# Rotary halves of the sparse and the odd block: exchanged by a signed permutation on TensorE, or by DMAs between rows

## The reference

```python
def apply_rope(x, cos, sin):
    half = x.shape[-1] // 2          # 32 of a head's 64
    x1, x2 = x[..., :half], x[..., half:]
    return jnp.concatenate([x1 * cos - x2 * sin, x2 * cos + x1 * sin], axis=-1)
...
q = apply_rope(rmsnorm(q.reshape(B, S, N_HEADS, HEAD_DIM), q_g), cos, sin)      # 16 heads
k = apply_rope(rmsnorm(k, k_g)[:, :, None, :], cos, sin)[:, :, 0]
qi = apply_rope(qi.reshape(B, S, IDX_HEADS, IDX_DIM), cos_i, sin_i)             # 8 index heads
ki = apply_rope(ki[:, :, None, :], cos_i, sin_i)[:, :, 0]
```

## Time and profile before

| | |
|---|---|
| median of 3 runs | 3494.64 us |
| lowest and highest | 3492.76, 3498.55 us |
| span of the profiled execution | 3495.7 us, 1.1 us above the median and within the runs |
| TensorE busy | 3254.3 us, 93% of the span |
| VectorE, ScalarE, GpSimd busy | 1721.7, 1278.4, 1177.5 us |
| mean granted TensorE clock | 0.969 of full speed |
| stage `dsa` | about 648 to 944 us of the span |
| stage `odd` | about 2720 to 2886 us of the span |

### The profile page before, as it was taken

One profiled execution on the slowest core, in us unless ns is written; L12 is line 12 of the kernel. 1 busy time (PEld: TensorE's weight loads), 2 busy tenths in 40 slices (PEclk: granted clock), 3 DMA queues, 4 the chain that ended last, 5 costly groups with the idle time before them and its releaser, 6 DMA issues.

```text
span 3495.7 us, 44614 instructions
## 1 busy us (share of the span) xinstructions
PE 3254.3 (93%) x18228; PEld 2555.2 (73%) x18228; DVE 1721.7 (49%) x3140; ACT 1278.4 (37%) x2273; POOL 1177.5 (34%) x963
## 2 busy tenths in 40 slices
PE   7999999887899997989899988999999998999998
PEld 3346888655678886755688876888887777868886
DVE  6754446588476676624566544122223318741223
ACT  2413223347432235625523234212113436743222
POOL 0233444542144442221265323223222342044443
PEclk9999999998999998999999999999999999999999
DMA  7513555310155542100122120111111111012221
GB/s 298 196 72 149 206 207 206 129 49 1 73 197 207 206 184 104 49 26 1 42 52 52 47 85 36 61 73 49 73 54 68 55 49 67 1 66 99 98 99 73
DMA packets 82412, 337.23 MB, mean 96 GB/s; under 512 B 46432, under 2 KB 50208, under 8 KB 57376
## 3 DMA queue, kind: packets, MB, share of 16 engines
q1 hardware_dynamic: 81344, 332.14, 25.7%
q10 hardware_dynamic: 864, 2.24, 0.2%
HBM read 326.64 MB, written 7.70 MB: 96 GB/s over the span
## 4 chain that ended last, share of the span: by engine, by line
PE 72%; DVE 14%; ACT 5%; POOL 3%; DMA 2%; issue 2%; SPq 1%; POOLq 0%; DVEq 0%; ACTq 0%
PE PSB L676 17%; PE PSB L680 17%; PE PSB L677 17%; PE PSB L1272 2%; PE PSB L1294 2%; PE PSB L1281 2%; PE PSB L563 2%; DVE SB L2064 2%; DVE SB L396 1%; DMA SB<-in_ada 1%; DVE SB L1366 1%; PE PSB L1833 1%; DVE PSB L1018 1%; DVE SB L1382 1%; DVE R L1024 1%
## 5 line engine op out<-in xcount | busy, mean ns | idle before, releaser
L680 PE MATMUL PSB<-R,WSR 128*128 128x512 f32 (+1 forms) x3084 | 1014.1, 366 | 0.0
L621 POOL TENSOR_TENSOR WSR<-SB,ahead 128x1024 fp32r<-128x1024 f32 x182 | 436.1, 2397 | 708.0 <-ACT ahead L598 672.6
L676 PE MATMUL PSB<-R,ahead 128*128 128x512 f32 (+1 forms) x1664 | 612.3, 368 | 2.5 <-POOL WSR L621 2.4
L677 PE MATMUL PSB<-R,ahead 128*128 128x512 f32 (+1 forms) x1664 | 592.7, 366 | 0.0
L680 PEld LDWEIGHTS PSB<-R,WSR 128*128 128x128 f32 x3084 | 533.0, 189 | 65.4
L676 PEld LDWEIGHTS PSB<-R,ahead 128*128 128x128 f32 x1664 | 312.9, 188 | 73.9 <-issue 3.5
L621 POOL TENSOR_TENSOR WSR<-SB,ffn_weights 128x1024 fp32r<-128x1024 f32 x96 | 230.0, 2396 | 388.7 <-ACT ffn_weights L598 388.7
L677 PEld LDWEIGHTS PSB<-R,ahead 128*128 128x128 f32 x1664 | 313.1, 188 | 52.8 <-issue 0.7
L676 PE MATMUL PSB<-R,ffn_weights 128*128 128x512 f32 x868 | 324.6, 374 | 7.2 <-POOL WSR L621 7.2
L677 PE MATMUL PSB<-R,ffn_weights 128*128 128x512 f32 x868 | 317.2, 373 | 0.0
L598 ACT ACTIVATE ahead<-SB 128x1024 fp32r<-128x1024 f32 x164 | 172.8, 1055 | 347.1 <-PE PSB L680 262.9
(11 more groups left out here) (441 smaller groups left out, 5763.1 us busy)
## 6 DMA issues: line engine op xcount, KB each, us to landing
SB<-in_w SPq DMA_DIRECT2D x95, 2048.0 KB, 7.5
SB<-in_ada SPq DMA_DIRECT2D x96, 1024.0 KB, 5.0
SB<-gate_rows SPq DMA_DIRECT2D x12, 512.0 KB, 4.0
SB<-in_rpb SPq DMA_DIRECT2D x8, 448.0 KB, 3.8
spill<-SB SPq DMA_DIRECT2D x1, 3072.0 KB, 9.6
SB<-gate_rows SPq DMA_DIRECT2D x24, 128.0 KB, 3.9
SB<-spill SPq DMA_DIRECT2D x1, 3072.0 KB, 9.9
SB<-in_x SPq DMA_DIRECT2D x8, 256.0 KB, 6.6
```

The lines of the kernel that those rows point to most:

```text
L621: e.tt(lr, t, hf, ALU.subtract).then_inc(*G.up(("lo", self.e0 + j)))
L676: e.mm(b[:, 0:n], wh, xh[:, lo:lo + n], x == 0, False)
L677: e.mm(b[:, 0:n], wh, xl[:, lo:lo + n], False, False)
L680: ins = e.mm(b[:, 0:n], wl, xh[:, lo:lo + n], False, last)
```

## The change

The permutation on TensorE goes, and with it the product or copy out of the bank. In its place SP issues four DMAs for each rotation, each of which copies 32 rows of the input tile (64 KB) to the partner's rows of `T`. The sign moves into the table of sines, which the host makes. `rot.dve` now multiplies `T` in place; in `dsa` from rotation 5 on POOL does it alone. `rot.pool` and `rot.dve` wait for the four DMAs to land. SP's program has the DMAs of rotation i between the calls of `panels`, and waits there until the input of the rotation is ready and until rotation i-2 is summed.

```diff
-        ropes += [np.cos(a4), np.sin(a4)]
+        ropes += [np.cos(a4), np.where(p[:, None] % 64 < 32, -1.0, 1.0) * np.sin(a4)]
...
         class Rotation:
-            def pe(self, e, P, i):
-                st = self.st
-                if i:
-                    e.wait_ge(*st.at("turn_sin", i - 1))
-                e.wait_ge(*self.ready(i))
-                e.mm(self.b, K["rot64"], self.xs[i][:, 0:S]).then_inc(*P.up(("turn", i)))
...
-            def act(self, e, A, i):
-                st = self.st
-                e.wait_ge(*st.at("turn", i))
-                if i >= len(self.T):
-                    e.wait_ge(*st.at("turned", i - len(self.T)))
-                e.act(self.T[i % len(self.T)], self.b, ACT.Copy).then_inc(*A.up(("turn_sin", i)))
...
+            def landed(self, i):
+                return self.swapped[i % len(self.T)], 64 * (i // len(self.T) + 1)
+
+            def sp(self, e, i):
+                st = self.st
+                e.wait_ge(*self.ready(i))
+                if i >= len(self.T):
+                    e.wait_ge(*st.at("turned", i - len(self.T)))
+                for o in range(0, 128, 64):
+                    for to, of in ((o, o + 32), (o + 32, o)):
+                        e.load(self.T[i % len(self.T)][to:to + 32, :], self.xs[i][of:of + 32, 0:S]).then_inc(
+                            self.landed(i)[0], 16)
+
+            def dve(self, v, D, i):
+                t = self.T[i % len(self.T)]
+                v.wait_ge(*self.landed(i))
+                v.tt(t, t, self.sin, ALU.mult).then_inc(*D.up(("turn_sin", i)))
+
+            def pool(self, e, G, i, alone=False):
+                st, x, t = self.st, self.xs[i][:, 0:S], self.T[i % len(self.T)]
+                e.wait_ge(*self.landed(i))
+                e.tt(x, x, self.cos, ALU.mult).then_inc(*G.up())
+                if alone:
+                    e.tt(t, t, self.sin, ALU.mult).then_inc(*G.up())
+                else:
+                    e.wait_ge(*st.at("turn_sin", i))
                 e.wait_ge(*G.now())
...
+                e.tt(x, x, t, ALU.add).then_inc(*G.up(("turned", i)))
...
@@ dsa, sp @@
-                for mt in order[:5] + [14] + order[5:]:
+                for s, mt in enumerate(order[:5]):
                     panels(e, "b_in", 7, mt)
-                for mt in range(8):
+                    rot.sp(e, s)
+                panels(e, "b_in", 7, 14)
+                for s, mt in enumerate(order[5:]):
+                    panels(e, "b_in", 7, mt)
+                    if s == 3:
+                        rot.sp(e, 5)
+                    if s >= 5:
+                        rot.sp(e, s + 1)
+                panels(e, "b_out", 7, 0)
+                for i in range(10, 14):
+                    rot.sp(e, i)
+                for mt in range(1, 8):
                     panels(e, "b_out", 7, mt)
...
@@ dsa, pe, att @@
-                    if i < 4:
-                        rot.pe(e, P, 10 + i)
                     if i == 3:
                         e.wait_ge(*st.at("head_ln", 8, 0))
-                    elif i == 4:
-                        e.wait_ge(*st.at("turn_sin", 13))
...
@@ odd, sp @@
                 for mt in range(14):
                     panels(e, "o_in", 7, mt)
+                    if mt >= 11:
+                        rot.sp(e, mt - 11)
                 for k in range(8):
                     panels(e, "nav", k, 0)
+                    if k in (0, 2, 4):
+                        rot.sp(e, 3 + k // 2)
```

More of the change, by code:

```diff
@@ L1444, in program, with __init__ @@
         class Rotation:
-            def __init__(self, st, bank, T, cos, sin, xs, ready):
-                self.st, self.b, self.T, self.cos, self.sin, self.xs, self.ready = st, bank, T, cos, sin, xs, ready
-            def pe(self, e, P, i):
+            def __init__(self, st, T, cos, sin, xs, ready):
+                self.st, self.T, self.cos, self.sin, self.xs, self.ready = st, T, cos, sin, xs, ready
+                self.swapped = [sem(f"{st.name}_swapped{j}") for j in range(len(T))]
+            def landed(self, i):
+                return self.swapped[i % len(self.T)], 64 * (i // len(self.T) + 1)
@@ L1451, in pe @@
+            def sp(self, e, i):
                 st = self.st
-                if i:
-                    e.wait_ge(*st.at("turn_sin", i - 1))
                 e.wait_ge(*self.ready(i))
-                e.mm(self.b, K["rot64"], self.xs[i][:, 0:S]).then_inc(*P.up(("turn", i)))
-            def dve(self, v, D, i):
-                st = self.st
-                v.wait_ge(*st.at("turn", i))
-                if i >= len(self.T):
-                    v.wait_ge(*st.at("turned", i - len(self.T)))
-                v.tt(self.T[i % len(self.T)], self.b, self.sin, ALU.mult).then_inc(*D.up(("turn_sin", i)))
@@ L1464, in act @@
-            def act(self, e, A, i):
-                st = self.st
-                e.wait_ge(*st.at("turn", i))
                 if i >= len(self.T):
                     e.wait_ge(*st.at("turned", i - len(self.T)))
-                e.act(self.T[i % len(self.T)], self.b, ACT.Copy).then_inc(*A.up(("turn_sin", i)))
-            def pool(self, e, G, i, copied=False):
-                st, x = self.st, self.xs[i][:, 0:S]
-                e.wait_ge(*st.at("turn", i))
+                for o in range(0, 128, 64):
+                    for to, of in ((o, o + 32), (o + 32, o)):
+                        e.load(self.T[i % len(self.T)][to:to + 32, :], self.xs[i][of:of + 32, 0:S]).then_inc(
+                            self.landed(i)[0], 16)
@@ L1476, in pool @@
                 e.wait_ge(*G.now())
-                e.wait_ge(*st.at("turn_sin", i))
-                if copied:
-                    t = self.T[i % len(self.T)]
-                    e.tt(t, t, self.sin, ALU.mult).then_inc(*G.up())
-                    e.wait_ge(*G.now())
-                e.tt(x, x, self.T[i % len(self.T)], ALU.add).then_inc(*G.up(("turned", i)))
+                e.tt(x, x, t, ALU.add).then_inc(*G.up(("turned", i)))
         def norm_dve(v, D, xs, n, H, lo, gs, u0):
@@ L1524, in dsa @@
                           HQ, HR)
-            rot = Rotation(st, banks[7], RT, RP[0], RP[1], [dst[t] for t in order],
+            rot = Rotation(st, RT, RP[0], RP[1], [dst[t] for t in order],
                            lambda i: st.at("evac", i) if i < 5 else st.at("normed", i - 5))
@@ L1573, in pe @@
                     e.mm(banks[4][0:72, :], wl[:, 0:72], H[k][1], False, k == 7).then_inc(*P.up(("vw_rows",), *used))
-                rot.pe(e, P, 4)
                 e.wait_ge(*st.at("vw_out"))
@@ L1652, in last_queries @@
                         hn.act(e, A, 7 + i)
-                    if i < 4:
-                        rot.act(e, A, 10 + i)
                     if i == 8:
@@ L3189, in odd @@
                           xs, SQ, RST)
-            rot = Rotation(st, banks[7], TR, RP[0], RP[1], xs, lambda i: st.at("normed", i))
+            rot = Rotation(st, TR, RP[0], RP[1], xs, lambda i: st.at("normed", i))
             rope_landed = sem("rope2_landed")
@@ L3229, in group_values_pe @@
             def group_values_pe(e):
-                e.wait_ge(*st.at("turn_sin", 5))
                 e.wait_ge(*st.at("head_ln", 5, 1))
@@ L3251, in pe @@
                         e.wait_ge(*st.at("h", 15))
-                    if s >= 3:
-                        rot.pe(e, P, s - 3)
                     if s >= 2:
@@ L3256, in pe @@
                     linear3(e, st, first[mt], ring, hv, "o_in", [mt], range(8), H, [(lo, n) for t, _, lo, n in groups if t == mt], ready)
-                rot.pe(e, P, 3)
                 hn.pe(e, P, 4)
```

14 lines of the change are left out of this document (removed).

## The result

The changed kernel takes 3517.8 us (median of 4 runs, 3515.5 to 3520.3), the kernel before 3495.6 us in the same comparison: the ratio is 1.0066, with an interval of 1.0054 to 1.0077. That is 22 us slower by the medians, 23 by the ratio; 11.6 were forecast, and 3517.8 lies 3.8 us above the range's end. The direction and the mechanism of rival A held; the forecast size was half of the measured one.

What follows compares the result with a forecast made beforehand. TensorE, busy 93% of the span and holding 72% of the chain, was taken as the bound. Terms +2.0 - 1.5 + 7.5 + 3.6 = +11.6 us on 3494.6 gave 3506 us, range 3496 to 3514.

Steps and rivals of the forecast that it cites:

- rival A: Whole kernel: row copies queue behind panels and POOL holds low weight parts behind them; 3506 us, 3498 to 3512; chance 0.62.
- `odd`, +11.1 us forecast with the clock: Two panels in `odd`: copies behind them delay projection 12 and neighbour values 4, +3.8 and +3.7 us, plus +3.6 for clock.
- the 256 KB of a rotation then need a quarter of 2.5 us, 0.65 us, behind the panel: `odd`, first panel: rotation 0's copies land 0.65 us behind the panel, at about 2809.9 us.
- The clock, +3.6 us forecast: `odd`: TensorE idles about 6 us before two steps; the lowered clock behind each costs 1.8 us, bounds 0 and 5.
- the 0.9 of permutation 2: `odd`, first panel: removing this permutation after projection 12 gives 0.9 us back.
- Front of `dsa`, +2.0 forecast: Start of `dsa`: copies delay the second panel by 2.3 us, and ReLUs, sums and search behind it; bounds -2.6 and +4.
- rotation 2 is summed at about 685.9 us, [...] and only then the second panel, at 687.5 us: Front of `dsa`: SP waits for that sum, issues rotation 4's four copies, then the panel, previously issued at 685.19 us.
- Start of the attention, -1.5 forecast: Attention's start in `dsa`: permutations and copies leave the chain, 0.86 + 0.61 us gained beyond what VectorE hides; bounds 0 and 3.4.
- Rival B: Row copies land 2.2 us after issue whatever stands before them; 3492 us, the same within what can be told; chance 0.17.
- C: TensorE's time comes back wherever the chain has it, in `dsa`, the attention and `odd`; 3484 us, faster; chance 0.08.
- D: Row copies are slow by themselves, 3.5 us or more each, in `dsa` and `odd`; 3510 us, up to 3514; chance 0.13.

Runs made afterwards that it cites:

- the kernel before with a gap: Kernel before the change, but GpSimd copies each of the two odd key tiles five times instead of once: 1.0066, +23 us.
- dsa-only kernel: The changed kernel with the odd layer keeping its permutation on TensorE, only the sparse layer using row DMAs: 1.0025, +8.7 us against the kernel before; repeated, 1.0027.

## Why the prediction was wrong

It named the right places and the right chain, and mis-sized their terms.

**`odd`, +11.1 us forecast with the clock, +17.5 measured alone, +17.3 in the trace.** The step that failed is "the 256 KB of a rotation then need a quarter of 2.5 us, 0.65 us, behind the panel". That priced a transfer by its bytes. Measured from the panel's issue, the copies landed after 9.8 and 11.6 us, not 8.15. The panel itself took 8.8 and 9.2 us and not 7.5, and the last copy landed 1.0 and 2.4 us behind it and not 0.65. That is 1.6 and 3.4 us of the 2.6 and 4.2 us by which projection 12 and values 4 came later than predicted. SP issues a row copy in 0.6 us where I had 0.33 to 0.45, so the last leaves 2.4 us behind the panel, but that is not what holds it: from 2805 to 2810 us every packet is of 16 KB, the panel's.

```profile
DMA packets 96, 1.57 MB, mean 315 GB/s; under 512 B 0, under 2 KB 0, under 8 KB 0
```

The rest, about 1 us each, is GpSimd: its three operations took 1.77, 1.52 and 2.78 us at the first panel, where the earlier trace rows have 1.29, 1.29 and 2.36. VectorE worked beside it; that VectorE slows it was not tried.

**The clock, +3.6 us forecast.** Right here: the two halves grew by 7.6 and 9.7 us, while the later starts of TensorE, 7.2 less the 0.9 of permutation 2, and 7.9, account for 6.3 and 7.9; what remains is 1.3 and 1.8. The windows behind the two gaps agree: 5.00 us of work at 0.67, in the row below, lose 1.7, and 3.21 at 0.50 with 5.00 at 0.95 behind the second gap lose 1.9.

```profile
2820.70:2825.70 5.00, 5.00 (x20) 0.67 0.06 14
```

It was right by luck of place. Had the second gap fallen 18 us later, ahead of the group values, it would by the kernel before with a gap have cost about 15 us more (an estimate: the 20.0 us there less the gap of 4.8). No case of the prediction had that.

**Front of `dsa`, +2.0 forecast.** Here the trace shows +7.1 at the end of the search, and the timed executions +5.2 for the first five rotations alone. The failed step is "rotation 2 is summed at about 685.9 us, [...] and only then the second panel, at 687.5 us". Counted from the stage's start, the first panel landed 4.2 us late, not 2.2 (issues of 0.6 us and more, and a longer flight), GpSimd's low parts took up to 2.88 us, and SP needed 2.5 us for four copies: 690.4. I had also taken the panel for the only bound. GpSimd's chain through rotation 4 and the scaling is about as late by itself: with the panel early the sum began 4.3 us later than before, counted from the stage's start, and 5.4 in the changed kernel.

**Start of the attention, -1.5 forecast.** The trace has -4.9 from the end of the search to the next stage (155.2 against 160.1 us), but this is not that term. With only the first five rotations changed, and the attention's start as before, the stretch is 155.5 us; with only the last nine changed it is 159.0. The shorter stretch goes with the late search and not with the nine rotations. The last nine alone measured +1.4 us, with an interval from -2 to +4.5. No run shows the forecast gain.

**Left open.** The dsa-only kernel costs 9 us when timed and 1.4 and 1.8 us by the next stage in its two profiles, both taken on its quickest execution (3496 and 3497 us, clock 0.970 and 0.968; the timed ones 3500 to 3513 at 0.961 to 0.967). Other traces narrow it. Seven traces have this same `dsa` (the changed kernel, dsa alone twice, and four of the runs on `odd`): there the stage takes 301.3 to 304.7 us, against 298.1 to 300.3 in the three that leave it as it was, 3.4 us more in the mean. With only the second panel put first, one execution of 3509 us was profiled; its `dsa` takes 307.5 us, 7.2 more than before. The stages between `dsa` and `odd`, which nothing touched, take from 1766 to 1780 us over all traces. So the stage itself carries 3 of the 9 us in the mean of the traces and 7 in that one execution, and what is left lies within what untouched stages vary by. Its cause stays open.

**Rival B** (no queue) is excluded by the landings, **C** (TensorE's time returned) happens in `odd` alone and only with one of the two orders mended, -3.0 or -4.0 us in the trace. **D** (slow copies) is wrong: copies with no panel about land in 2.0 us.

## What to carry to other kernels

Before a small transfer goes to a queue of large ones, look at what is in flight on the DMA engines, not at its own size or queue: 64 KB landed in 2.0 us just ahead of a 2 MB panel, and in 6 to 9 us just behind it, in the same queue or another. And where a consumer works in order (GpSimd here), ask which of the things behind the waiting one has the nearest deadline, and put it ahead.

Price an idle stretch of TensorE by what follows it, and look at the granted clock there: 9.5 us ahead of matmuls of 512 columns cost 2 us beyond themselves, 4.8 us ahead of matmuls of 128 columns cost 15.

When a fix moves the expected wait and the time stays, read the halves apart: one run here gained 10 us and lost 7 further on in one trace.

## What the runs showed of the hardware

- After 2.91 and 4.76 us of idle time, 144 matmuls of 128 columns ran at a granted clock of 0.50, busy all the time, for about 30 us; it did not come back during them. Without the gap the same matmuls ran at 1.00 and took some 16 us. Behind 9.48 us of idle time, matmuls of 512 columns brought it back in some 4 us. Which property of the matmuls makes the difference was not tried.
- A DMA between rows of SBUF (32 rows of 2 KB) takes SP 0.6 us to issue and lands in 2.0 us alone. Issued within 3 us behind a 2 MB panel it lands in 6.3 to 9.1 us in the same queue and in 6.0 to 7.7 in another; issued 4 to 6 us behind one, in another queue, in 3.8 to 5.0.
- The panel took longer too: 8.8 and 9.2 us with copies behind it in its queue and 8.2 with copies in another, 7.7 and 7.5 in the same two places of `odd` before.
